# Second MLP of a three-part transformer step on one Trainium2 core: its second matrix by seven block products in three quarters, squares of the relu on ScalarE

## The reference, cut to what matters

```python
def sq_relu_mlp(h, w1, w2):                     # w1: 1024 x 4096, w2: 4096 x 1024
    return jnp.square(jax.nn.relu(h @ w1)) @ w2
# layer i of the first block, after its mixer:
    h = modulate(rmsnorm(x, norm_mlp_g[i]), sh2, sc2)
    x = x + g2[:, None, :] * sq_relu_mlp(h, mlp_w1[i], mlp_w2[i])
# second block, last part:
    return (jax.nn.gelu(gate, approximate=True) * val) @ w_down    # w_down: 4096 x 1024
```

## Time and profile before

| | us |
|---|---|
| median of 3 runs | 1795.23 (1794.46 to 1796.09) |
| profiled execution, its own time | 1799.05 |
| its span | 1797.1 |
| PE busy | 1747.5 (97%) |
| DVE busy | 1099.4 (61%) |
| ACT busy | 675.4 (38%) |
| POOL busy | 86.5 (5%) |
| DMA | 124 GB/s in the mean |

### The profile page before, as it was taken

The page is one execution under the profiler, slowest core; times in us unless marked ns, Lnnn a source line. Parts: engine busy times, 40 slices in busy tenths (PEclk is TensorE's granted clock), DMA queues, the critical chain, the costliest instruction groups (busy, mean ns, idle before and its releaser), DMA issues. The chain is left out here.

```text
span 1797.1 us, 22643 instructions
## 1 busy us (share of the span) xinstructions
PE 1747.5 (97%) x9353; PEld 1416.8 (79%) x9353; DVE 1099.4 (61%) x1363; ACT 675.4 (38%) x833; POOL 86.5 (5%) x102
## 2 busy tenths in 40 slices
PE   7899999999999999999999998999999999999997
PEld 4378888888788788888888786777888888888885
DVE  4475774477455543234346667675668668578578
ACT  4343113411333333124234633444444344344344
POOL 0100110010000000000000011120000000000000
PEclk9899999999999999999999998999999999999999
DMA  9942662266222232222222232002343444336324
GB/s 369 355 156 94 234 233 95 94 234 223 83 94 71 81 106 95 94 94 94 94 96 98 77 94 65 8 2 95 129 121 91 155 115 141 118 94 181 101 71 128
DMA packets 131445, 223.34 MB, mean 124 GB/s; under 512 B 14493, under 2 KB 49973, under 8 KB 131344
## 3 DMA queue, kind: packets, MB, share of 16 engines
q1 hardware_dynamic: 118736, 182.28, 30.5%
q0 software_dynamic: 12464, 39.04, 7.6%
q10 hardware_dynamic: 144, 0.59, 0.1%
HBM read 218.72 MB, written 4.73 MB: 124 GB/s over the span
## 5 line engine op out<-in xcount | busy, mean ns | idle before, releaser
L1975 DVE TENSOR_TENSOR w_lo<-raw,w_hi 128x2048 fp32r<-128x2048 f32 x116 | 265.9, 2292 | 349.6 <-ACT w_hi L1444 349.4
L1444 ACT ACTIVATE w_hi<-raw 128x2048 fp32r<-128x2048 f32 x120 | 229.5, 1912 | 485.4 <-PE bank L674 451.5
L674 PE MATMUL bank<-h_hi,w_hi 128*128 128x512 f32 x736 | 290.5, 395 | 6.9 <-DVE h_lo L2022 2.9
L674 PE MATMUL bank<-h_hi,w_lo 128*128 128x512 f32 x736 | 287.5, 391 | 0.0
L674 PE MATMUL bank<-h_lo,w_hi 128*128 128x512 f32 x736 | 287.4, 391 | 0.0
L674 PE MATMUL bank<-u_hi,w_hi 128*128 128x512 f32 x512 | 200.8, 392 | 0.0
L674 PE MATMUL bank<-u_hi,w_lo 128*128 128x512 f32 x512 | 199.4, 389 | 0.0
L674 PE MATMUL bank<-u_lo,w_hi 128*128 128x512 f32 x512 | 199.2, 389 | 0.0
L674 PE MATMUL bank<-f_hi,w_hi 128*128 128x512 f32 x496 | 193.0, 389 | 0.0
L674 PE MATMUL bank<-f_lo,w_hi 128*128 128x512 f32 x496 | 193.0, 389 | 0.0
L674 PE MATMUL bank<-f_hi,w_lo 128*128 128x512 f32 x496 | 192.9, 389 | 0.0
(11 more groups left out here) (414 smaller groups left out, 2536.9 us busy)
## 6 DMA issues: line engine op xcount, KB each, us to landing
raw<-in_mlp_w SPq DMA_DIRECT2D x128, 512.0 KB, 4.6
ada_ring<-in_ada_w SPq DMA_DIRECT2D x12, 2048.0 KB, 14.4
ada_ring<-in_ada_w POOLq DMA_DIRECT2D x24, 1024.0 KB, 5.6
raw<-in_w_ffn_up SPq DMA_DIRECT2D x32, 512.0 KB, 5.0
raw_more<-in_w_ffn_up SPq DMA_DIRECT2D x32, 512.0 KB, 4.9
raw<-in_w_in SPq DMA_DIRECT2D x20, 512.0 KB, 4.7
raw<-in_w_ffn_down SPq DMA_DIRECT2D x20, 512.0 KB, 4.7
raw_more<-in_w_ffn_down SPq DMA_DIRECT2D x20, 512.0 KB, 4.7
```

What stands on the lines that cost most here:

```text
L674: mm = te.matmul(bank[:, n], a, b, start=first and k == 0 and j == 0, stop=last and k == 3 and j == 2, skip_group_check=s == SLABS["ffn"] + 1)
L1444: se.activation(m.ring(s)[0], m.raw_place(s), ACT.Copy).then_inc(sem("hi_made"), 1)
L1975: ve.tensor_tensor(lo, m.raw_place(s), hi.bitcast(F32), ALU.subtract).then_inc(sem("lo_made"), 1)
```

## The change

- **Second MLP in quarters.** Each of four quarters makes 8 hidden tiles by four slabs of w1. In quarters 0 to 2, w2 then goes by the FFN's seven products (the helpers take a `stage` argument now), with sums into its own `f`, `u`, blocks and `raw_more`. In quarter 3, w2 goes as before, by two groups of two slabs with transposed result.
- **Token rows turned back.** The sums of quarters 0 to 2 lie with tokens in partitions. In quarter 3, between tiles of its first group, PE transposes them (32 transposes of 128 x 128, `rows_back`) into banks 4 to 7, and DVE adds them to `xT` (`rows_mixed`, 8 instructions).
- **Squares on ACT.** In the second MLP ACT writes the relu to `u` and squares it there; in quarter 3 it also rounds it.
- **Raw places.** The second MLP has four raw places. The first loads into places 2 and 3 wait until all slabs before it are used. The second MLP has 41 slabs now, two of which are summed on DVE in each of three quarters, so the raw places of later slabs change parity: the first slab of the FFN now waits for the split of the last slab of w_out, not of the one before.
- **Order in `products_lo`**, for both stages: update y stands ahead of the split of a22, no longer behind it.
- **POOL** issues the second MLP's twelve accumulating DMAs, ahead of its wait for the slabs before `proj`.

The core of the diff:

```diff
-SLABS = {"mlp0": 0, "sgu_in": 32, "sgu_out": 40, "mlp1": 44, "proj": 76, "w_out": 86, "ffn": 90}
+SLABS = {"mlp0": 0, "sgu_in": 32, "sgu_out": 40, "mlp1": 44, "proj": 85, "w_out": 95, "ffn": 99}
+QUARTERS = {"mlp1": 3, "ffn": 4}
+UP_SLABS = {"mlp1": 4, "ffn": 8}
 def raw_slot(s):
-    return s % 2 if s < SLABS["ffn"] else (s - SLABS["ffn"]) % 4
+    stage = stage_of(s)
+    return (s - SLABS[stage]) % 4 if stage else s % 2
...
@@ SP
+        if slot >= 2 and s == SLABS["mlp1"] + slot:
+            sy.wait_ge(sem("slab_used"), SLABS["mlp1"])
...
@@ PE
+    def rows_back(o):
+        te.wait_ge(sem("f_updated"), update_count("mlp1", QUARTERS["mlp1"] - 1, "p4"))
+        if o >= 4:
+            te.wait_ge(sem("x_mixed"), 8 + o - 3)
+        for n in range(4):
+            mm = te.transpose(bank[:, 4 + o % 4, P * n:P * n + P], m.quartered["mlp1"].f[:, n, P * o:P * o + P], ident)
+        mm.then_inc(sem("x_turned"), 1)
+    def mlp1(norm):
...
+        for q in range(4):
+            for g in range(2):
+                group, s = g0 + 2 * q + g, stage_slab("mlp1", q, 2 * g)
+                for k in range(2):
+                    def before_n(n):
+                        if g or not q:
+                            emptied(group - 1, n)
+                        else:
+                            te.wait_ge(sem("f_updated"), update_count("mlp1", q - 1, "p2" if n < 2 else "p4"))
...
+                    slab(s + k, group, m.h_hi[:, 4 * k:4 * k + 4], m.h_lo[:, 4 * k:4 * k + 4], k == 0, k == 1,
+                         before_k if q + g == 0 else None, before_n, after_n=after_n)
+                    if q == plain and g + k == 0:
+                        after_n(3)
+            if q < plain:
+                products("mlp1", q, g0 + 2 * q + 1)
+        for g in range(2):
+            group, s = g0 + 8 + g, stage_slab("mlp1", plain, 4 + 2 * g)
...
@@ ACT, quarters 0 to 2 of mlp1
+                if q < plain and g:
+                    block_hi("mlp1", q, "b11")
+                    block_hi("mlp1", q, "t1")
+                split_to(s + 2)
+                relu(0)
+                relu(1)
+                squared(0)
+                squared(1)
...
+                relu(2)
+                if q < plain and g:
+                    block_hi("mlp1", q, "b21_0")
+                    squared(2)
+                    block_hi("mlp1", q, "t2_0")
+                    split_to(s + 3)
+                    relu(3)
+                    squared(3)
...
+            if q < plain:
+                products_hi("mlp1", q)
+                split_to(stage_slab("mlp1", q + 1, 1))
@@ DVE
+    def products_lo(stage, q, beside=None):
+        split_to(product_slab(stage, q, "a12"))
+        block_lo(stage, q, "b21_1")
+        t3(stage, q, 1)
+        t2(stage, q, 1)
+        update(stage, q, "p1")
+        split_to(product_slab(stage, q, "s2"))
+        block_lo(stage, q, "t2_1")
+        update(stage, q, "p5")
+        block_lo(stage, q, "b22")
+        split_to(product_slab(stage, q, "s4"))
+        block_lo(stage, q, "t3")
+        update(stage, q, "u2")
+        t4(stage, q)
+        split_to(product_slab(stage, q, "s3"))
+        update(stage, q, "p2")
+        block_lo(stage, q, "t4")
+        if beside:
+            beside()
+        update(stage, q, "y")
+        split_to(product_slab(stage, q, "a22"))
+        update(stage, q, "u3_22")
+        update(stage, q, "u3_21")
...
+                if q < plain and g:
+                    t1("mlp1", q)
+                    block_lo("mlp1", q, "b11")
+                    block_lo("mlp1", q, "t1")
+                    s2("mlp1", q)
+                split_to(s + 2)
+                if q < plain and g:
+                    s4("mlp1", q)
+                    t3("mlp1", q, 0)
+                    block_lo("mlp1", q, "b21_0")
+                    t2("mlp1", q, 0)
+                    block_lo("mlp1", q, "t2_0")
+                elif q == plain:
+                    if g == 0:
+                        for o in range(8):
+                            rows_mixed(o)
+                    for n in range(4):
+                        low(4 * g + n)
+                split_to(s + 3)
+            if q < plain:
+                products_lo("mlp1", q)
+                split_to(stage_slab("mlp1", q + 1, 0))
+                update("mlp1", q, "p4")
+                split_to(stage_slab("mlp1", q + 1, 1))
@@ FFN on DVE, before
-        if q == QUARTERS - 1:
-            ve.wait_ge(sem("last_g_in"), 16)
-            last_gained(0, 0)
-            last_gained(0, 1)
-        split_to(product_slab(q, "a22"))
-        update(q, "y")
@@ POOL
+    for q in range(QUARTERS["mlp1"]):
+        add("mlp1", q, "s1", 1, 1)
+        add("mlp1", q, "s3", 1, 0)
     ge.wait_ge(sem("slab_used"), SLABS["proj"])
```

More of the change, by code:

```diff
@@ new lines, in product_of, with quarter, raw_before @@
+def product_of(s):
+    stage = stage_of(s)
+    if stage is None:
+        return None, None, None
+    q, j = divmod(s - SLABS[stage], UP_SLABS[stage] + len(PRODUCTS))
+    j -= UP_SLABS[stage]
+    return stage, q, PRODUCTS[j] if j >= 0 and q < QUARTERS[stage] else None
+def quarter(stage, q):
+    return QUARTERS_BEFORE[stage] + q
+def raw_slot(s):
+    stage = stage_of(s)
+    return (s - SLABS[stage]) % 4 if stage else s % 2
+def raw_before(s):
+    earlier = [r for r in range(s) if raw_slot(r) == raw_slot(s)]
+    return max(earlier) if earlier else None
@@ L452, in ring @@
         hi, lo = self.rings[0 if s < SLABS["w_out"] else 1 if s < SLABS["ffn"] else 2]
-        return hi[s % 2], lo[s % 2]
+        slot = s % 2 if s < SLABS["w_out"] else (s - SLABS["w_out"]) % 2
+        return hi[slot], lo[slot]
     def raw_place(self, s):
         slot = raw_slot(s)
[L458 to L470, removed]
+        return self.raw[:, slot] if slot < 2 else self.quartered[stage_of(s)].raw_more[:, slot - 2]
     def block(self, u):
@@ L509, in linear, with products, mlp_quartered @@
         return [[(slice(0, 512), block(w, k0 + k, slice(512 * g, 512 * g + 512)))] for g in groups for k in range(kslabs)]
+    def products(stage, q):
+        blocks = {"a11": (0, 0), "s1": (1, 0), "a12": (0, 1), "s3": (0, 0), "a22": (1, 1)}
+        return [[] if name in SUMMED_HERE else [(slice(0, 512), down_block(t, stage, q, *blocks[name]))] for name in PRODUCTS]
+    def mlp_quartered():
+        w1, w2 = t["mlp_w1"][1], t["mlp_w2"][1]
+        out = []
+        for q in range(4):
+            out += linear(w1, 2, (2 * q, 2 * q + 1))
+            out += products("mlp1", q) if q < QUARTERS["mlp1"] else linear(w2, 2, range(2), 2 * q)
+        return out
     def mlp(layer):
@@ L518, in ffn @@
         out = []
-        for q in range(QUARTERS):
+        for q in range(4):
             for i in range(4):
@@ L524, in ffn @@
                                 for v in range(2)])
[L525 to L527 removed]
+            out += products("ffn", q)
         return out
[L530 removed]
+    out = mlp(0) + linear(t["sgu_w_in"], 2, (2, 3, 0, 1)) + linear(t["sgu_w_out"], 2, range(2)) + mlp_quartered()
     out += linear(t["w_in_2"], 2, range(5)) + linear(t["w_out_2"], 2, range(2)) + ffn()
```

685 lines of the change are left out of this document (393 added, 292 removed).

## The result

The changed kernel took **1784.83 us** (median of four runs, 1781.88 to 1786.81) beside 1795.66 for the kernel before: 0.9938, interval 0.9920 to 0.9955, 10.8 us less. Over all its twelve timed runs in this study the median is 1782.26, over 39 of the kernel before 1795.88: 13.6 us less.

The account below looks back on a forecast made before the run. PE's matmuls bound the second MLP, 0.2267 us each. Matmuls -16.3, transposes +3.5 and update y -0.85 sum to -13.7 us: 1795.2 becomes 1781.5 us, forecast's own range 1780 to 1783, 8 in 10 within 1779.8 to 1785.5.

Parts of the forecast that it names:

- The matmuls: Second MLP: 1464 matmuls instead of 1536, 72 fewer at 0.2267 us each, -16.3 us.
- The transposes: Quarter 3 of the second MLP: 32 in four batches of eight, 0.88 us per eight, +3.5 us, no stall.
- Dear transposes: Rival: each transpose costs its whole 0.28 us, 9.0 instead of 3.5 us, time 1787.0; chance 0.05.
- The entry to the products: Second MLP, up slabs to products: s1 ready with 0.6 us room, cost 0; if DVE or ACT lags, 0.4 to 1.4 us a quarter.
- The sums of weights: POOL's adds to s3 in the second MLP land just in time: 0, range 0 to 5 us over three quarters.
- the prediction's own sign of being wrong: ACT's split of s3 starting over 23 us after a11, or PE waiting over 1 us a quarter for s1, s3 or a22.
- The rival of late operands: Thin margins fail at s3's adds (5 us in all) or the products' entry (up to 4 us): 1783.5 to 1788; chance 0.14.
- Starved adds, the slower side: Rival: DVE's work slows POOL's adds, s3 lands late, PE stalls 6.8 us a quarter, kernel ends at 1802; chance 0.03.
- Squares on ACT: Second MLP: moving the relu's squares from DVE to ACT changes nothing in PE's time, as both engines idled; 0.
- First loads and the FFN's first slab: Loads at the second MLP's start and the FFN's first raw load, waiting for a w_out split, stay hidden: 0.
- Update y: FFN's last quarter: y ahead of a22's split leaves two updates behind it, end earlier by 0.85 us, bounds +0.2 and -1.15.

Follow-up runs that it names:

- the hold: Changed kernel, but SP loads a22 and what is behind it only when POOL's two adds to s3 have landed, second MLP and FFN; alone a single 1784.79 us.

## Why the prediction was right

It said 1781.5, 13.7 us below the runs of before. Measured were 1784.83 in the first four runs, inside the range of 1779.8 to 1785.5 but above the forecast's own 1780 to 1783, and a difference of 13.6 between the medians of all runs. That the two agree to 0.1 us is partly luck: single terms below are off by up to 0.5 us, and the medians of the changed kernel's three groups of runs lie from 1780.05 to 1784.83. Step by step:

- **The matmuls, -16.3.** Three product stretches of 38.11, 38.12 and 38.46 us, quarters of 81.64 and 81.98, and 90.62 for the last (forecast 38.1, 81.6 and 90.6). Without the transposes the stage would have fallen by 16.2: 358.52 less 342.35.
- **The transposes, +3.5.** 3.58 by leaving them out. "Dear transposes" (9.0) is refuted. The Trainium skill, "TensorE: Matmul & The Clock Gate", "PE-mode transpose", gives about 275 ns for one in a kernel; as a duration it agrees with the rows' 0.28, as a price it would be refuted with that rival.
- **The entry to the products, 0.** s1 was 0.7 us early (forecast 0.6), a22 0.5 (0.6), a12's block 0.3 (0.5). The last was a misreading: the prediction counted from 1496.06, a start in the chain of waits. In PE's timeline a11's first matmul is at 1495.90, so all its margins in the FFN were 0.16 us too wide, and a12's block was 0.3 us early there too. With squares on DVE ahead of it s1 was still 0.7 early.
- **The sums of weights, 0, range 0 to 5.** In the second MLP of the three profiled executions of the changed kernel 0.34, 0 and 0 us. The FFN, for which the prediction had taken the trace of before as proof that four quarters run through, lost 0, 0.83 and 0.74 us in its quarter 1. There the prediction's own sign of being wrong, a split of s3 over 23 us behind a11, was met twice (23.44 and 23.35), in the second MLP never. The rival of late operands is thus real, and its size is under 1 us a run. Its threshold, 22.9 us, was predicted to 0.1 us; the way to it had two errors that offset each other. The issue was taken from quarter 1 of the FFN, the latest of the four (11.4 us behind a11; the others 9.9 to 10.2), while the second MLP's came at 10.2 to 10.3 and the second add 0.7 us behind the first, not 1.2. And the median landing of 8.4 us mixes first and second adds: s3 waits for the second, and in the second MLP that landed 10.8 to 11.9 us behind its issue, 21.8 to 22.9 behind a11. So the usual case already lies 1 us from the threshold. That behind a long pause the clock falls was not in the prediction either.
- **Starved adds, the slower side.** The gain was to be used up when ACT's split starts 4.6 us beyond the threshold. With the issue delayed by 6.8 us it started 4.2 to 5.5 us beyond, and the kernel was slower than before (one run, 1803.12 us). What lengthens the landing is in the main other DMA traffic: with the hold the second add landed 8.2 us behind its issue in the second MLP, not 10.8 to 11.9, with DVE's work unchanged. Whether DVE's work adds something to the rest is open: the squares moved back to DVE lie outside the time in which the adds to s3 are in flight.
- **Squares on ACT, 0.** Shown by moving them back.
- **First loads and the FFN's first slab, 0.** DVE's idle time ahead of the w_lo of the FFN's first slab is 8.20 us in both kernels, and that w_lo starts 16.0 us ahead of the FFN's first matmul in both.
- **Update y, -0.85, bounds +0.2 and -1.15.** Measured -1.06 with the change and -1.16 alone: L2946 came 1.08 us earlier. From the first gains on it is as forecast: a22's split starts 2.34 us behind them, not 2.16, and one update of 1.13 fewer stands behind it, together -0.95. The last 0.1 is that those gains themselves began 0.1 us earlier against the FFN's start. The term was 0.2 to 0.3 us too small.
- **Outside the span.** Device time less span was 1.84 us before (1.6 to 2.0) and 1.3 in every run with the changed second MLP (1.27 to 1.37 in the changed kernel). These 0.5 us were in no step; moving y alone left them. Their cause is open.

The profiled executions differ by 17.2 us, 3.6 more than the runs' medians; 3.1 of that are the two stretches that the change does not touch. In both it is the clock, as far as the traces show a cause. First the stage before the FFN: PE by stretch over the same 40 us, counted from the second MLP's end (PE busy and its matmuls, then PEclk, DMA share, GB/s), for the kernel before, the one with squares on DVE, and the one with the hold:

```profile
1094.75:1134.75 40.00, 37.50 (x446) 0.90 0.07 11
```

```profile
1078.39:1118.39 40.00, 37.35 (x474) 0.96 0.07 11
```

```profile
1080.00:1120.00 40.00, 37.21 (x420) 0.87 0.10 24
```

From the second MLP's end to the FFN these took 314.28, 312.23 and 316.59 us, with nothing changed in that stage: the lower the granted clock, the fewer matmuls in the same 40 us and the longer the stage.

The first MLP's start (76.58 and 74.11 us) goes the same way. Of these 2.5 us, 1.1 lie in 29 transposes of the input, before and changed:

```profile
17.94 6.26 PE L788 MATMUL bank<-const,x_rows 128*128 128x128 f32 x29 [0.72 <-DMA x_rows<-in_x]
```

```profile
17.73 5.14 PE L878 MATMUL bank<-const,x_rows 128*128 128x128 f32 x29 [0.77 <-DMA x_rows<-in_x]
```

They start 0.21 us apart before, and in the changed kernel the last twelve 0.11 apart. Another 1.1 us lie near 66 us, where PEclk is 0.50 for 6.8 us before and for 3.4 in the changed kernel. In the other profiles the first MLP starts at 73.1 to 74.3 us with the changed second MLP and at 74.65 with y alone moved; that the two profiles with the old second MLP start latest is not explained.

## What to carry to other kernels

Price a stage by the distance between its instructions, and let the same form elsewhere in the trace stand for the new one: here that gave 12.8 us for a measured 12.6. Take starts from the engine's timeline, not from the chain of waits, and look at every quarter of the form, not at one. Where several DMAs are waited for, read the landing of the last, not a median over all. Then look for the transfer that lands last with no room, put a number on the room, and delay it on purpose to check it; a hold on the plain loads that fly beside it gave back 9.8 of the 9.9 us that a late issue had cost. A difference of 1 us in runs that scatter by 3 to 7 has to be read from the spans of stages, not from the time.

## What the runs showed of the hardware

- Accumulating DMAs kept the DMA engines full at half of what plain loads reached. With the hold, the adds of quarter 1 of the FFN alone in flight (columns of the earlier trace rows; the last two are DMA share and GB/s):

```profile
1496.50:1500.50 4.00, 4.00 (x19) 3.24 (x18) 3.93 (x3) 2.87 (x5) 0.00 (x0) 1.00 1.07 193
```

  Plain loads at the same share, in the changed kernel:

```profile
1502.50:1506.50 4.00, 4.00 (x19) 3.34 (x18) 3.91 (x3) 2.96 (x2) 0.00 (x0) 1.00 1.07 380
```

  Against the profile with the hold alone, the plain loads in flight with the adds to s3 made the second one land 2.6 to 3.7 us later in the second MLP's three quarters.
- Pauses of PE of 4.2 to 5.5 us (three) were each followed by 5.6 to 5.9 us of matmuls at 1.2 GHz (granted clock 0.50). Of three pauses of 2.4 to 2.7 us one was followed by 3.4 us of them; pauses of 0.3 to 0.8 us never were.
- A multiplication of 128 x 512 took POOL 1.29 us. Beside DVE instructions with two SBUF inputs one engine waited until the other's instruction had ended: POOL's took 3.14 us beside w_lo, DVE's gain 1.86 instead of 0.69 beside POOL's. DVE's updates out of PSUM were not slowed.
